# Pair turns of a two-block transformer kernel: scores in one block, values groups in one block

## The reference, cut to what matters

```python
o_a = _dsa_attention(heads(qa), heads(ka), heads(va), qi, ki, wi, slopes)   # causal, top 64 keys, distance slopes
o_b = _forgetting_attention(heads(qf), heads(kf), heads(vf), log_f)         # causal, running forget sums
o_c = _stick_breaking_attention(heads(qs), heads(ks_), heads(vs))           # strict, running products
branches = jnp.stack([o_a, o_b, o_c], axis=0)
up = jnp.einsum('ibsw,iwd->bsid', branches, w_branch[layer])
g = jax.nn.sigmoid(gates.reshape(b, s, N_BRANCHES, D_MODEL))
merged = jnp.sum(up * g, axis=2)
y = jnp.einsum('bsd,de->bse', merged, w_out[layer])
```

## Time and profile before

| What | Value |
|---|---|
| median of 3 runs (lowest, highest) | 1364.0 us (1363.79, 1364.14) |
| span of the profiled execution, first to last instruction | 1362.3 us |
| what lies around the span, by the median of the runs (the page gives no time of its own for this execution) | 1.7 us |
| PEld, DVE, ACT busy | 1210.5 (89%), 1044.2 (77%), 797.6 us (59%) |
| DMA | 227.80 MB, mean 167 GB/s |

### The profile page before, as it was taken

How to read it: one execution, slowest core, us unless ns; L and a number is a source line. 1 busy time by engine, 2 the same in 40 slices (tenths; PEclk the granted TensorE clock), 3 DMA queues, 4 the chain that set the end, 5 groups by cost and what they waited for, 6 DMA issues and landing times.

```text
span 1362.3 us, 24396 instructions
## 1 busy us (share of the span) xinstructions
PE 1348.9 (99%) x8590; PEld 1210.5 (89%) x8590; DVE 1044.2 (77%) x1644; ACT 797.6 (59%) x1352; POOL 29.4 (2%) x72
## 2 busy tenths in 40 slices
PE   8999999999999999999999999999999999999998
PEld 8888888989888888888899999999999998988887
DVE  5798888777666686666778898898898877666665
ACT  4445554644334364444668898898898853544444
POOL 6000000000000010000000000000000000000000
PEclk9999999999999999999999999999999999999999
DMA  8565555556555756666564444554543286666661
GB/s 267 153 194 153 149 147 160 190 194 206 185 185 187 226 150 209 186 185 185 155 183 136 132 123 131 135 148 115 149 131 123 88 211 203 173 205 197 191 186 62
DMA packets 291214, 227.80 MB, mean 167 GB/s; under 512 B 10882, under 2 KB 270164, under 8 KB 291156
## 3 DMA queue, kind: packets, MB, share of 16 engines
q1 hardware_dynamic: 291012, 226.75, 56.0%
q10 hardware_dynamic: 144, 0.26, 0.1%
HBM read 225.90 MB, written 1.08 MB: 167 GB/s over the span
## 4 chain that ended last, share of the span: by engine, by line
PE 93%; DVE 3%; ACT 1%; issue 1%; DVEq 1%; ACTq 0%; DMA 0%; POOL 0%; SPq 0%; POOLq 0%
PE M L2119 10%; PE G L2119 9%; PE M L2107 7%; PE M L2108 7%; PE M L2109 7%; PE G L2102 5%; PE G L2104 5%; PE G L2103 5%; PE M L2121 5%; PE G L2121 5%; PE G L2245 2%; PE G L3007 2%; PE M L2830 1%; PE M L2812 1%; PE G L3009 1%; PE G L2109 1%
## 5 line engine op out<-in xcount | busy, mean ns | idle before, releaser
L1241 DVE TENSOR_TENSOR w_lo<-w_raw,w_hi 128x2048 fp32r<-128x2048 f32 (+2 forms) x247 | 478.0, 1941 | 126.4 <-ACT w_hi L655 120.6
L655 ACT ACTIVATE w_hi<-w_raw 128x2048 fp32r<-128x2048 f32 x197 | 375.9, 1909 | 169.5 <-PE M L2121 54.3
L2102 PE MATMUL G<-xa,w_hi 128*128 128x256 f32 x592 | 176.9, 299 | 0.0
L2104 PE MATMUL G<-xa,w_lo 128*128 128x256 f32 x592 | 167.3, 283 | 0.0
L2103 PE MATMUL G<-xa,w_hi 128*128 128x256 f32 x592 | 167.0, 282 | 0.0
L2119 PE MATMUL M<-xa,w_hi 128*128 128x512 f32 x600 | 151.6, 394 | 0.0
L2119 PE MATMUL G<-xa,w_hi 128*128 128x512 f32 x568 | 142.4, 393 | 0.0
L2119 PEld LDWEIGHTS M<-xa,w_hi 128*128 128x128 f32 x600 | 107.8, 189 | 19.8
L2119 PEld LDWEIGHTS G<-xa,w_hi 128*128 128x128 f32 x568 | 104.0, 188 | 21.2 <-issue 1.2
L2107 PE MATMUL M<-w_hi,xb 128*128 128x512 f32 x300 | 117.3, 391 | 0.1
L2108 PE MATMUL M<-w_lo,xb 128*128 128x512 f32 x300 | 117.1, 390 | 0.0
(11 more groups left out here) (461 smaller groups left out, 2545.2 us busy)
## 6 DMA issues: line engine op xcount, KB each, us to landing
w_raw<-in_w_in SPq DMA_DIRECT2D x150, 512.0 KB, 4.7
w_raw<-in_ffn_w_in SPq DMA_DIRECT2D x88, 512.0 KB, 5.0
w_raw<-in_w_ff SPq DMA_DIRECT2D x64, 512.0 KB, 4.1
w_raw<-in_ffn_w_out SPq DMA_DIRECT2D x44, 512.0 KB, 4.9
w_raw<-in_w_in SPq DMA_DIRECT2D x33, 256.0 KB, 3.2
w_raw<-in_w_out SPq DMA_DIRECT2D x16, 512.0 KB, 4.1
w_raw<-in_w_branch_gdn SPq DMA_DIRECT2D x16, 512.0 KB, 5.3
w_raw<-in_w_branch SPq DMA_DIRECT2D x12, 512.0 KB, 4.2
```

What stands on the lines that cost most here:

```text
L655: nc.scalar.activation(w_hi[:, slot, :], w_raw[:, slot, :], ACT.Copy).then_inc(hi_ready, 1)
L1241: return v.tensor_tensor(dst, src, hi.bitcast(F32), ALU.subtract)
L2102: mm(out_, w[0], x[0], start=first, stop=False)
L2104: return mm(out_, w[1], x[0], start=False, stop=last_)
```

## The change

In a turn of the loop, PE does not run the first branch's scores behind `pair_wide(2)` and the second's behind chunk 3; it runs both between the two halves of chunk 3, after waiting for both sums of DVE. The values of the first and third branch go from behind `gate_wide(4)` to behind `gate_wide(5)`, ahead of those of the second branch. ACT's `o_hi` and DVE's `o_low` for these two branches follow: on ACT behind the second `pt_copy` and the last `split`, on DVE behind the gate sums and the last `w_low`, in the order 0, 2, 1. In the branch stage the chunks of branch 0 use G and not M's first two banks; the first of them runs its first three quarters before it waits for the last pair's result, and the others are as they were.

```diff
@@ ACT, a turn @@
             split(c0 + 4 + RING, p, 6)
-            o_hi(2, 4, p)
-            o_hi(0, 0, p)
             pt_copy(1, 2, pt_f, p)
             split(c0 + 5 + RING, p, 6)
+            o_hi(0, 0, p)
+            o_hi(2, 4, p)
             o_hi(1, 2, p)
@@ DVE, a turn @@
             w_low(c0 + 4 + RING, p, 6)
-            o_low(2, 4, p)
-            o_low(0, 0, p)
             gate_sum(4, p)
             gate_sum(5, p)
             w_low(c0 + 5 + RING, p, 6)
+            o_low(0, 0, p)
+            o_low(2, 4, p)
             o_low(1, 2, p)
@@ DVE, branch stage @@
-                up = M[:, 2 * i:2 * i + 2, :].rearrange("p b c -> p (b c)")
+                up = (G if i == 0 else M[:, 2 * i:2 * i + 2, :]).rearrange("p b c -> p (b c)")
@@ PE, a turn @@
             pair_wide(2, p)
-            copied(1, p)
-            scores(0, 0, qa_t, ka_t, p)
-            pair_chunk(3, p, col_gemm)
-            copied(2, p)
-            scores(1, 2, qf_t, kf_t, p)
+
+            def both_scores():
+                copied(1, p)
+                copied(2, p)
+                scores(0, 0, qa_t, ka_t, p)
+                scores(1, 2, qf_t, kf_t, p)
+
+            pair_chunk(3, p, lambda slot, bank: col_gemm(slot, bank, between=both_scores))
...
             gate_wide(4, p, lambda: prob_t(0, 0, log_a, p))
             pe.wait_ge(pt_ready[0], p + 1)
+            gate_wide(5, p, lambda: prob_t(1, 2, log_fo, p))
             pe.wait_ge(va_ready, p + 1)
             values(0, 0, va_p[:, 0, :], va_p[:, 1, :], pt_a)
             pe.wait_ge(stick_ready, p + 1)
             values(2, 4, vfs[:, 0, P:T], vfs[:, 1, P:T], st2)
-            gate_wide(5, p, lambda: prob_t(1, 2, log_fo, p))
             pe.wait_ge(pt_ready[1], p + 1)
             values(1, 2, vfs[:, 0, 0:P], vfs[:, 1, 0:P], pt_f)
@@ PE, branch stage @@
-            if n < 3:
-                pe.wait_ge(ol_ready[i], PAIRS + 1)
-            else:
-                pe.wait_ge(branch_used, n - 2)
+            if n >= 3:
+                pe.wait_ge(branch_used, n - 2)
+            elif n > 0:
+                pe.wait_ge(ol_ready[i], PAIRS + 1)
...
+            banks = G if i == 0 else M[:, 2 * i:2 * i + 2, :]
...
+            if n == 0:
+                for j in range(4):
+                    if j % 2 == 0:
+                        pe.wait_ge(evac[j // 2], EV_FF[j // 2])
+                    tile_steps(j, range(3), False)
+                pe.wait_ge(ol_ready[0], PAIRS + 1)
+                for j in range(4):
+                    ins = tile_steps(j, (3,), False)
+            else:
+                for j in range(4):
+                    ins = tile_steps(j, range(4), True)
```

More of the change, by code:

```diff
@@ L2469, in _, with tile_steps @@
             weights_ready(c0 + n)
-            if n < 3:
+            if n >= 3:
+                pe.wait_ge(branch_used, n - 2)
+            elif n > 0:
                 pe.wait_ge(ol_ready[i], PAIRS + 1)
-            else:
-                pe.wait_ge(branch_used, n - 2)
             wh = w_hi[:, slot, :].rearrange("p (k c) -> p k c", c=512)
             wl = w_lo[:, slot, :].rearrange("p (k c) -> p k c", c=512)
[L2476 to L2482, removed]
+            banks = G if i == 0 else M[:, 2 * i:2 * i + 2, :]
+            def tile_steps(j, ks, whole):
+                out_, at = banks[:, j // 2, T * (j % 2):T * (j % 2) + T], slice(P * j, P * j + P)
+                for k in ks:
+                    first = k == 0 and (whole or j % 2 == 0)
+                    x = (xb_hi[:, 4 * i + k, :], xb_lo[:, 4 * i + k, :])
+                    mm(out_, wh[:, k, at], x[0], start=first, stop=False, skip_group_check=not whole)
+                    mm(out_, wh[:, k, at], x[1], start=False, stop=False, skip_group_check=not whole)
+                    ins = mm(out_, wl[:, k, at], x[0], start=False, stop=k == 3, skip_group_check=not whole)
+                return ins
+            if n == 0:
[9 more added lines that the diff above has]
+                    ins = tile_steps(j, range(4), True)
             ins.then_inc(gemm_done, 1)
```

## The result

The changed kernel takes 1365.86 us (median of 21 runs), the kernel before in the same measurement 1363.91 us: 1.95 us more, ratio 1.0015 with a 95% interval of 1.0009 to 1.0021. The forecast was 2.1 us more. The profiled execution took 1365.5 us with a span of 1363.7.

What follows compares the result with a forecast made beforehand. PE was taken to bound the kernel, with DVE's and ACT's softmax chain limiting each turn once its cover goes. 0.65 + 3 x 0.50 = +2.15 us on 1364.0 gave 1366.1 us, range 1363.4 to 1367.4.

Steps and rivals of the forecast that it cites:

- What bounds: Whole kernel: PE is in flight 99% of the span; only what makes PE start a matmul earlier or later counts.
- The scores' block: Middle of chunk 3: joining saves 0.27 us, PE stalls about 0.4 on pair_sum(2), later starts 0.15 late, normalise(1) unmoved.
- the slack: DVE ahead of the st2 product: a 0.45 us wait for ACT, room for the steps behind the late addition.
- The values' block: Behind gate 5: PE stalls 0.6 us at second transposes; turn moves -0.95 + 0.05 + 1.40 = +0.50 us.
- The first turn: Loop's first turn: PE starts second transposes 0.80 us earlier; -0.80 + 0.05 + 1.40 = +0.65 us.
- the sum: Loop's four turns: 0.65 + 3 x 0.50 = +2.15 us.
- Moves at no cost: o_hi and o_low moved on ACT and DVE: covered, cost nothing; without that cover, 0.4 us per subtraction and turn.
- (a): Rival, loop: the switches decide and PE never stalls; each turn saves 0.58 us, 1361.7 us in all; chance 0.12.
- (b): Rival, second transposes: cover only half gone as DVE's chain gains; about 0.5 us better per turn, 1364.0; chance 0.10.
- (c): Rival, scores: the copied(2) wait delays later over 0.45 us, pushing normalise(0) and st2; 1368.1 us; chance 0.10.

Runs made afterwards that it cites:

- e5: Changed kernel, but the first branch chunk waits for the last pair's o_low(0) before its first matmul; median 4.1 us above the changed kernel's.
- e2: Changed kernel with the scores left as before, so the values part alone; costs what the whole change costs, to 0.1 us.
- e8: Changed kernel with DVE reordered: row_max(1), normalise(1), pair_sum(2), gate sums earlier, chunk 2's weight subtraction behind row_max(0); 2.84 us under before, ratio 0.9979.
- e10: Kernel before with the scores joined and DVE's pair_sum(2) ahead of the forget-mask subtractions; turn 0.14 us under before.
- e11: Changed kernel with scores as before, DVE's normalise(1) chain shortened and gate sums ahead of chunk 4's weight subtraction; turn 0.33 us under before.

## Why the prediction was right

- **What bounds.** Right: the branch stage and everything behind it kept their length, and the whole difference lies in the four turns.
- **The scores' block.** The stall was put at 0.4 us, the idle column shows 0.44. `later` starts 8.04 us behind the end of `pair_wide(2)` (225.10 to 233.14); I had 7.92. The missing 0.12 is mostly the restart behind that wait, 0.16 us from DVE's end to the first scores, for which I allowed none. It did not matter, as I said it would not, but not for the reason that I gave. The `st2` sum came 0.19 us later against the chain. What took that up is a wait of 0.18 us right behind it, for the first softmax's exponentials on ACT, which I had not counted:

```profile
234.33 0.18 DVE L1378 RECIPROCAL arena<-arena 128x4 f32<-128x4 f32 x1 [0.18 <-ACT arena L742]
```

In the profile after, the same reciprocal at 235.39 has no wait and stands 7.26 us behind the `pair_sum(2)` scaling, as before. The 0.45 us wait ahead of the `st2` product, which I had named as the slack, is 0.45 in both traces.
- **The values' block.** The forecast step was: PE reaches the second transposes 0.6 us before their data. It was 0.57. A group between two others was priced at 0.70; the rows after have 0.70 and 0.65, 1.34 us more per turn when the exit (0.80 against 0.81) is counted in. A turn is 0.45 us longer, and I had 0.50: the group in the middle, 0.65 where I took 0.70 as the least, is the mis-sized term.
- **The first turn.** +0.65 was forecast, +0.48 measured (42.27 to 42.75 between the third branch's scores). Its chain on ACT and DVE hangs on the landing of a weight chunk, and this came 0.15 us earlier against the loop's start than in the trace of before: 11.58 us behind it and not 11.73 (79.64 to 91.22, before 79.94 to 91.67). First before, then after:

```profile
91.67 1.92 ACT L655 ACTIVATE w_hi<-w_raw 128x2048 fp32r<-128x2048 f32 x1 [4.05 <-DMA w_raw<-in_w_in]
```

```profile
91.22 1.91 ACT L655 ACTIVATE w_hi<-w_raw 128x2048 fp32r<-128x2048 f32 x1 [3.90 <-DMA w_raw<-in_w_in]
```

I read the first turn's end of `normalise(1)` as fixed, when a DMA set it. This and the middle group make the loop's +1.81 where the sum gave +2.15; that the medians differ by 1.95, nearer to the forecast, is luck: the interval of the ratio, 1.2 to 2.9 us, holds all three.
- **Moves at no cost.** `o_low` ended at 252.84, no branch matmul waited for it, and the trace of e5 prices that cover at a wait of 2.6 us, where I said 2.5; in four of the five runs of e5 it cost about 1.6 us more, unexplained. The next turn waits for no `o_low` either.
- **Rivals.** (a), the switches decide, fell with e2, but its size was nearly right: 0.58 us per turn worked out, 0.64 in e8, whose loop is free of waits. What it lacked was not the saving but someone to bring the probabilities forward. (b) fell too: DVE's chain gained nothing. (c) did not happen, and was further off than I thought: 0.45 of room in my sum, 0.18 + 0.45 in the rows, of which the trace used 0.19. Going into and out of the half-array groups once less saves 0.31 us for the scores and 0.33 for the values (e10, e11); that a drain of the array is what takes this time, no run shows. The saving alone would have forecast the wrong sign.

## What to carry to other kernels

When work is moved on the bounding engine, ask first what that work was covering: the values groups were 1.7 us of cover for a softmax on two other engines, and joining them for 0.3 us of saving cost 0.6 us of waiting. Here a joined block paid only together with an earlier arrival of what the engine meets next, and each gain on PE moved the limit to the next such meeting (second transposes, scores, gate sum, first transposes, in turn). A busy share of 99%, which PE had before and after, says nothing of such waits; distances between starts do.

## What the runs showed that I had not expected

PE's restart behind a wait was not the same at the two places: 0.05 us from the end of DVE's product to a transpose over 128 rows, 0.16 us from the end of the scaling to scores over 64 rows. The entry into the scores took 0.10 us before too, where nothing was waited for (224.03 to 224.13 in the earlier trace rows); whether that is the difference was not tested. And of three values groups in a row the middle one takes 0.65 us, less than the first's 0.70.
